# Whole 14 KB weight rows for the wide expert jobs of a one-core decoder trunk

## What is computed

```python
def swiglu(h, wg, wu, wd):
    return (jax.nn.silu(h @ wg) * (h @ wu)) @ wd

def moe_swiglu(h, router_w, wg, wu, wd):
    logits = (h @ router_w).astype(jnp.float32)
    top_val, top_idx = lax.top_k(logits, TOP_K)
    top_w = jax.nn.softmax(top_val, axis=-1)
    gates = jnp.sum(jax.nn.one_hot(top_idx, N_EXPERTS, dtype=jnp.float32) * top_w[..., None], axis=-2).astype(h.dtype)
    y = jnp.zeros_like(h)
    for e in range(N_EXPERTS):
        y = y + gates[..., e:e + 1] * swiglu(h, wg[e], wu[e], wd[e])
    return y
```

## Time and profile before

| | us |
|---|---|
| median of 3 runs | 1389.39 |
| lowest, highest | 1388.88, 1390.56 |
| the profiled execution, its own time | 1389.21 |
| its span, first to last instruction | 1387.4 |
| PE busy | 1370.8 (99%) |
| DVE busy | 806.9 (58%) |
| ACT busy | 663.1 (48%) |
| DMA read | 452.69 MB, 327 GB/s over the span |

### The profile page before, as it was taken

The page is one execution under the profiler, slowest core; times in us unless marked ns, Lnnn a source line. Parts: engine busy times, 40 slices in busy tenths (PEclk is TensorE's granted clock), DMA queues, the critical chain, the costliest instruction groups (busy, mean ns, idle before and its releaser), DMA issues.

```text
span 1387.4 us, 17886 instructions
## 1 busy us (share of the span) xinstructions
PE 1370.8 (99%) x6681; PEld 942.6 (68%) x6681; DVE 806.9 (58%) x1142; ACT 663.1 (48%) x886; POOL 10.3 (1%) x22
## 2 busy tenths in 40 slices
PE   9999999999999999999999999998999999999997
PEld 8887788888898877743435788434788535788432
DVE  5878666545458786631123999323899423999311
ACT  7657646444376485500012788212787212787210
POOL 2000000000000000000000000000000000000000
PEclk9999999999999999999999999999999999999999
DMA  9545446555544477899999999999999999999997
GB/s 352 194 173 183 154 144 220 182 187 194 176 156 160 159 273 284 310 404 426 406 429 420 422 422 426 430 431 420 421 422 429 430 430 420 421 423 428 430 429 296
DMA packets 105539, 454.91 MB, mean 328 GB/s; under 512 B 6440, under 2 KB 8752, under 8 KB 83696
## 3 DMA queue, kind: packets, MB, share of 16 engines
q1 hardware_dynamic: 104528, 452.47, 81.6%
q0 software_dynamic: 752, 1.23, 0.4%
q10 hardware_dynamic: 176, 0.07, 0.0%
HBM read 452.69 MB, written 1.06 MB: 327 GB/s over the span
## 4 chain that ended last, share of the span: by engine, by line
PE 87%; DMA 6%; DVE 3%; ACT 3%; issue 1%; DVEq 0%; ACTq 0%; SPq 0%
PE pA L841 39%; PE pB L841 19%; PE pB L1375 10%; PE pA L1375 8%; PE pA L1437 4%; DMA toep<-expert_w_gate_dram 4%; DMA late<-expert_w_down_dram 2%; PE pB L865 2%; PE pA L865 1%; DVE w_lo L1893 1%; ACT w_hi L1532 1%; PE pA L1294 0%; PE pB L1073 0%; ACT early_hi L1532 0%; PE pB L1254 0%
## 5 line engine op out<-in xcount | busy, mean ns | idle before, releaser
L1893 DVE TENSOR_TENSOR w_lo<-raw,w_hi 128x1024 fp32r<-128x1024 f32 x236 | 280.8, 1222 | 71.8 <-ACT w_hi L1532 68.9
L1532 ACT ACTIVATE w_hi<-raw 128x1024 fp32r<-128x1024 f32 x236 | 243.9, 1059 | 77.9 <-PE pB L841 38.5
L1893 DVE TENSOR_TENSOR w_lo<-late,w_hi 128x1024 fp32r<-128x1024 f32 x126 | 150.0, 1223 | 11.7 <-ACT w_hi L1532 6.0
L1532 ACT ACTIVATE w_hi<-late 128x1024 fp32r<-128x1024 f32 x126 | 132.4, 1061 | 33.0 <-PE pB L841 20.5
L1844 ACT ACTIVATE ex_act<-pA 64x512 f32<-64x512 f32 x15 | 8.9, 591 | 259.7 <-PE pA L1375 212.2
L1893 DVE TENSOR_TENSOR early_lo<-raw,early_hi 128x1024 fp32r<-128x1024 f32 x58 | 69.8, 1221 | 34.7 <-ACT early_hi L1532 34.6
L1375 PE MATMUL pB<-late,x_narrow 128*64 128x512 f32 x296 | 81.7, 592 | 0.0
L841 PE MATMUL pB<-w_hi,jT_hi 128*128 128x512 f32 x192 | 76.3, 397 | 2.5 <-DVE w_lo L1893 2.4
L2394 DVE TENSOR_TENSOR x<-pA,x 128x512 f32<-128x512 f32 x16 | 11.1, 692 | 116.2 <-PE pA L1295 116.2
L841 PE MATMUL pA<-w_hi,hT_hi 128*128 128x512 f32 x192 | 77.1, 402 | 0.0
L841 PE MATMUL pB<-w_hi,jT_lo 128*128 128x512 f32 x192 | 75.4, 393 | 0.0
(11 more groups left out here) (464 smaller groups left out, 2718.0 us busy)
## 6 DMA issues: line engine op xcount, KB each, us to landing
late<-expert_w_down_dram SPq DMA_DIRECT2D x46, 1024.0 KB, 19.8
raw<-w_in_dram SPq DMA_DIRECT2D x43, 1024.0 KB, 4.9
late<-expert_w_up_dram SPq DMA_DIRECT2D x29, 1024.0 KB, 18.4
first_run<-expert_w_gate_dram SPq DMA_DIRECT2D x16, 1792.0 KB, 16.0
first_run<-expert_w_up_dram SPq DMA_DIRECT2D x16, 1792.0 KB, 16.8
late<-expert_w_gate_dram SPq DMA_DIRECT2D x16, 1792.0 KB, 17.0
late<-expert_w_up_dram SPq DMA_DIRECT2D x16, 1792.0 KB, 17.7
raw<-expert_w_gate_dram SPq DMA_DIRECT2D x27, 1024.0 KB, 19.7
```

Of the source, the lines that this page charges most:

```text
L1532: f(halves_slot(m)[0], raw_slot(m), ACT.Copy).then_inc(s["w_hi_done"], 1)
L1893: tt(lo, raw_slot(m), hi.bitcast(F32), ALU.subtract).then_inc(s["w_lo_done"], 1)
```

## The change

Wide jobs take the same transfers as narrow ones, with all gate rows first, then all up rows, then the downs. The two lists come from one function, `job_items`. The piece order is written out by `wide_pieces`: for the gate matrix rows 0 to 3 in pairs (for each row the column pairs 0-1, 2-3, 4-5, then column chunk 6 of both rows as one piece of two runs of 512), then columns 0-1 of rows 4 to 7, then the rest of these rows in pairs; the same for up; then 28 down pieces. All seven gate sums stand in seven banks at once (B3, B1, B4, B5, B6, B7, B0), all seven Silu results in SBUF (six in the new `wide_acts` of 12 KB per partition, which lies over `low_slots` and `low_half`, used by job 0 alone, and the seventh in `ex_act`), and the up products take the same banks. Silus run at pieces 17, 19, 25, 25, 26, 27, 28, products at 45, 47, 53, 57, 59, 61, 63, transposes at 50, 57, 60, 64, 68, 72, 76. The scatter of the job before goes in four parts at pieces 8, 12, 16 and 20 through B2 alone, with the additions at 10, 14, 18 and 22. A ring place is free for the next load when the last piece of both rows of its pair is split. The cut diff:

```diff
+def job_items(narrow):
+
+    order = [("up" if r % 2 else "gate", r // 2) if narrow else ("up" if r // KT else "gate", r % KT) for r in range(ROWS)]
+    rows = [(unit, r // RUN_ROWS // 2, r // RUN_ROWS % 2, r % RUN_ROWS, r % RUN_ROWS * ROW, ROW)
+            for r, unit in enumerate(order)]
...
+def wide_pieces():
+
+    out = []
+    for kind in ("gate", "up"):
+        for k in range(0, RUN_ROWS, 2):
+            out += [(kind, k + r, c) for r in range(2) for c in (0, 2, 4)] + [(kind, k, SINGLE)]
+        out += [(kind, k, 0) for k in range(RUN_ROWS, KT)]
+        for k in range(RUN_ROWS, KT, 2):
+            out += [(kind, k + r, c) for r in range(2) for c in (2, 4)] + [(kind, k, SINGLE)]
+    return out + [("down", d // 4, d % 4) for d in range(4 * (FE // COLS))]
...
+        wide_acts = run_of.enter_context(nc.sbuf_tensor("wide_acts", [P, FE // COLS - 1, COLS], F32))
...
+        TURN_AT = [WIDE_ROWS - 6, WIDE_ROWS + 1, *(WIDE_ROWS + 4 * (c - 1) for c in range(2, SINGLE + 1))]
+        SILU_AT = [pieces.index(("gate", KT - 1, 0)) + n for n in (0, 2, 8, 8, 9, 10, 11)]
+        PRODUCT_AT = [pieces.index(("up", KT - 1, 0)) + n for n in (0, 2, 8, 12, 14, 16, 18)]
+
+        def w_bank(c):
+            return (B3, B1, B4, B5, B6, B7, B0)[c]
...
-                    sp.wait_ge(s["w_lo_done"], EX0 + FFE * wide_before(owner) + 2 * (RING * before + RUN * run + places[-1]) + 2)
+                    if before == 2:
+                        last = WIDE_ROWS + 2 * (RUN * run + places[-1]) + 1
+                    else:
+                        kind, k = items[False][RUN_ROWS * (2 * before + run) + (at + size - 1) // ROW][0]
+                        last = pieces.index((kind, k // 2 * 2, SINGLE))
+                    sp.wait_ge(s["w_lo_done"], EX0 + FFE * wide_before(owner) + last + 1)
...
-                if j and is_narrow(j):
-                    for (kind, c, *n), at_pass, run, slot, at, size in items:
+                if j:
+                    for (kind, c, *n), at_pass, run, slot, at, size in items[is_narrow(j)]:
...
             def job(j, w):
                 pe.wait_ge(s["n_x_ready"], w + 4)
                 pe.wait_ge(s["spread_ready"], j + 1)
...
+                for t, (kind, k, c) in enumerate(pieces):
+                    m = EX0 + t
                     if kind == "gate":
...
+                        pe.wait_ge(s["xg_lo_done"], 4 * w + k // 2 + 1)
+                    if kind == "up" and k < 2:
+                        pe.wait_ge(s["silu_done"], D0 + NCX * w + min(c + 2, NCX))
...
+                    elif c == SINGLE:
+                        chunk_piece(m, k // 2, COLS, [w_bank(c)], jT_hi, jT_lo, 1, j=w)
+                    else:
+                        row_piece(m, k, k == 0, [[w_bank(c), w_bank(c + 1)]], jT_hi, jT_lo, 1, w)
...
+                    if t in (8, 12, 16, 20):
+                        n = (8, 12, 16, 20).index(t)
+                        scatter_half(j - 1, n // 2, n % 2, False, 1)
```

More of the change, by code:

```diff
@@ L92, in ffn_order @@
     return order, at
[L95 to L107, removed]
 FOUR, TWO, SINGLE = (0, 1, 2, 3), (4, 5), 6
@@ L384, in program @@
         assert RING_SLOTS[PHASE] == ("toep", 0)
-        items = narrow_items()
-        item_at = {unit[:2]: place[:3] for unit, *place in items}
+        items = [job_items(narrow) for narrow in (False, True)]
+        item_at = [{unit[:2]: place[:3] for unit, *place in of_job} for of_job in items]
+        pieces = wide_pieces()
+        assert len(pieces) == FFE
         def ring_slot(kind, k):
@@ L407, in once_slot, with in_halves, unit_slot, unit_half @@
             return {"ex": once_ex, "ga": once_ga, "acts": once_acts}[name][:]
[L409 to L415, removed]
+        def in_halves(u):
+            return u in once and ONCE[once[u][0]][0] == "halves"
+        def unit_slot(u):
+            if u in once:
                 return once_slot(u)
-            return ring_slot(*RING_SLOTS[(ring_of_first[u] if first else PHASE + u) % RING])
-        def unit_half(u, h, first):
-            if in_halves(u, first):
+            return ring_slot(*RING_SLOTS[ring_of_first[u] % RING])
+        def unit_half(u, h):
+            if in_halves(u):
                 return (low_half, once_y)[h][:]
-            return unit_slot(u, first)[:, PIECE * h:PIECE * (h + 1)]
+            return unit_slot(u)[:, PIECE * h:PIECE * (h + 1)]
+        def wide_raw(t):
+            kind, k, c = pieces[t]
+            if kind == "down":
+                u = 2 * k + c // 2
+                return run_part(u // RUN, u % RUN * UNIT + PIECE * (c % 2), PIECE)
+            at_pass, run, slot = item_at[False][kind, k]
+            if c == SINGLE:
+                both = run_part(run, slot * ROW, 2 * ROW).rearrange("p (r n) -> p r n", r=2)
+                return both[:, :, COLS * SINGLE:]
+            return run_part(run, slot * ROW + COLS * c, PIECE)
+        def like_raw(m, part):
+            if m >= EX0 and pieces[m - EX0][2] == SINGLE and pieces[m - EX0][0] != "down":
+                return part.rearrange("p (r n) -> p r n", r=2)
+            return part
         def raw_slot(m):
@@ L476, in program @@
         assert n == FFD
[L477 to L478 removed]
+        assert len(EXPERT_W) == SINGLE + 1
         def ends(order):
@@ L491, in turns, with wide_act @@
             return at
[L493 to L519, removed]
+        TURN_AT = [WIDE_ROWS - 6, WIDE_ROWS + 1, *(WIDE_ROWS + 4 * (c - 1) for c in range(2, SINGLE + 1))]
[3 more added lines that the diff above has]
+            return (B3, B1, B4, B5, B6, B7, B0)[c]
+        def wide_act(c):
+            return ex_act[:, 0] if c == SINGLE else wide_acts[:, c]
         def turn_bank(c):
-            return (B6, B7)[c % 2] if c else B4
+            return (B1, B4)[c % 2]
         def load_pair_count(eng):
```

162 lines of the change are left out of this document (60 added, 102 removed).

## The result

The changed kernel takes **1405.08 us** (median of four runs, 1403.87 to 1416.04) against 1389.48 (1388.88 to 1390.56) before: a ratio of 1.0129, with a 95% interval of 1.0078 to 1.0180. It is 15.6 us slower where 2.5 us less was predicted. The run of 1416.04 had a mean granted clock of 0.944, the other three 0.995 to 0.996. The profiled execution took 1405.76 us, with a span of 1404.0.

A forecast was written before the change was run, and what follows sets the result against it. DMA (208.0 us a pair of jobs) was taken to bound, PE almost level (204.94). Start +1.7 less 1.3 of waits gives +0.4; less 2.9, -2.5 on 1389.21, plus 0.18 to the median: 1386.9 us, range 1383.3 to 1390.5.

The forecast's parts named there:

- The start of a wide job: First wide job waits for whole rows 0 and 1: +1.13, +0.2 and +0.4, together +1.7 us, paid once.
- PE in a wide job: Matmul and transpose counts in wide jobs unchanged, so 0 us, bounds -0.5 to +0.5.
- Covered: Scatters at pieces 8 to 20 share one bank; 1.36 x 2 us are left for an addition's 1.06 + 0.69.
- The loads: Wide jobs' weights come in 103.0 us instead of 105.0, 2.0 us a job; last weights land 6.0 us earlier.
- Removable waits: PE's waits for down weights, 1.3 us in the first narrow job and 2.9 in the last: 4.2 us.
- The loop's gap stays: The 2.42 us gap ahead of the second wide job belongs to PE's loop branch, not weights, and remains.
- The low clock stays: Granted clock of 0.60 for 4 us behind the loop's gap remains; that wide job is 1.56 us longer.
- Rivals 1 and 2: Loop gap ahead of second wide job: 1 shrinks with slow clock, 1383.5 us, 11%; 2 grows by 1.7, 1388.6 us, 15%.
- ACT and DVE: In wide jobs the same operations at moved places: 0 us, bounds -0.2 to +2 us a job.
- rival 3: ACT becomes the bound at pieces 25 to 33 and 57 to 63: +5.7 us, 1392.6 us, chance 11%.
- Release by pairs: A slot's next load waits for both rows of a pair; queue stays filled, cost 0, bounds 0 to 2 us.
- Rival 4: Larger rows bring nothing: wide jobs' loads stay at 105.0 us, total 1389.5 us, chance 8%.

The follow-up runs named there:

- e1_order: Changed kernel with rows 4 and 5 of gate and up taken as a pair, columns 0-1 ahead only for rows 6 and 7; 1388.79 us.
- e2_scatter_late: Changed kernel with its own piece order, scatters moved to pieces 29, 33, 37, 41 and additions to 31, 35, 39, 43; 1407.27 us.
- e3_short_rows: Changed kernel loading only the first quarter of the columns of gate rows 4 to 7 in each wide job; 1388.69 us.
- e7_paired_scatter: Changed kernel in e1_order's piece order, both scatter halves side by side in two banks after pieces 23 and 25; 1385.38 us.
- e4_quarter_runs: e1_order with each wide gate and up row loaded as four transfers of 3.5 KB runs; 1390.20 us.
- e6_before_light: Kernel before, with half of each wide down weight not loaded; 1382.69 us.
- e5_all_pairs: Changed kernel with all eight rows in pairs, no columns ahead, Silus and products moved to suit; 1403.04 us (two runs).
- e8_three_ahead: e7_paired_scatter with three pieces, not four, split ahead of the copy of the narrow job's output; 1385.04 us.

## Why the prediction was wrong, step by step

- **The start of a wide job (+1.7): near at its place, and stopped too early.** Worked out were +1.13 for PE's first matmul, +0.2 and +0.4; measured are +1.73 for the first matmul (760.69 where 760.09 was worked out) and 0.4 at piece 3, 2.1 in all. The kernels with the new loads start between 759.92 and 760.72, so part of the difference is spread. But the step followed the landing of rows 0 and 1 only. Its own numbers were enough to see the stall. With row 0 at 757.71 and 4.27 us a row, row 6 lands at 783.3 and is ready 2.38 later, at 785.7; row 7 at 787.6 and 790.0. PE, started at 760.09, is through sixteen pieces of 1.36 at 781.9, or 783.6 with two scatter halves of 0.89 (measured), and wants row 6 there, 2.1 us too early; it wants row 7 one piece and one half on, at 785.9, 4.1 us too early. The trace has PE at row 6's piece at 786.38 and at row 7's at 793.20. Of the 7.3 us lost in this job these numbers give 4.1 and the low clock 1.5; the rest I don't divide further (ACT's copy of row 7 begins at 789.14 where 787.6 was worked out, and DVE's addition goes ahead of the scatter). **This is the step that failed**: it took the wait for rows 4 to 7 at nothing, and 17.3 us hang on it, more than the 16.6 of the whole (after against e1_order, 7.3 + 2.1 + 7.9; e2_scatter_late and e3_short_rows bear out the cause).
- **PE in a wide job (0, bounds -0.5 to +0.5): wrong, +1.75 us a job, 5.2 in the sum.** "No term changes" counted scatter matmuls, eight before and after, not the places where they interrupt the pieces: two before, four after, at 0.76 + 0.13 us each. e7_paired_scatter takes 1.7 us back in each of the first two jobs. The prediction's "Covered" for the scatters at 8 to 20 holds for the waits where rows are on time (e1_order has none there), but not for the scatters themselves; and in the change the addition that piece 16's scatter needs stood behind a subtraction for row 7, which the 1.06 + 0.69 us of that sum left out.
- **The loads (2.0 us a job): right.** Wide loads run at 430 GB/s once PE keeps up (e1_order, 752.5 to 857.5 us), at 416 to 420 with 3.5 KB runs (e4_quarter_runs). Within the change they only reached 408 from 765 to 855 us, for want of free places. (The slices at 9 tenths begin at 590 us, 17 of 34.7, and not at 622 as the prediction has it; nothing hangs on it.)
- **Removable waits (4.2 us): mis-sized.** 6.0 us in e6_before_light's span. After also got all of it: narrow jobs and the end gave back 6.5 us. Six waits of the brackets hid 1.9 us more, 0.3 each.
- **The loop's gap stays: right. The low clock stays: wrong in this profile,** which gives 1.6 us back. The branch takes 5925 ns in after and 5825 to 6301 in the experiments, the gap 1.9 to 2.4 us. Rivals 1 and 2 both fall as they were put: of rival 1 only the low clock's part came, and the gap is 2.02 where it was 2.42.
- **ACT and DVE (0), and rival 3: right that it costs nothing.** PE has no wait at pieces 25 to 33 or 57 to 67 in any kernel but e5_all_pairs, whose order delays the products. The slower side came by another way than the one rival named for it.
- **Release by pairs (0 us, and the queue stays filled): the cost is right, the reason is not.** The prediction named a DMA share under 1.0 about 1090 us as a sign that the queue runs dry. It came, in after (0.95 from 1096 to 1112 us) and in e1_order, where there is no stall:

```profile
1084.00:1100.00 16.00, 16.00 (x74) 8.66 (x75) 5.42 (x6) 3.59 (x5) 0.00 (x0) 1.00 0.94 378
```

  The kernel before has 430 GB/s in the same 16 us, and its shortest time from issue to landing there is 11.9 us, e1_order's 8.2. So the queue did run low behind the second wide job, and that narrow stage came at 419 GB/s in place of 428 (1065.5 to 1168.5 us). It cost PE nothing: no matmul waits in it. e7_paired_scatter, with the same release, has 407 GB/s there, and e6_before_light, with the old one and fewer bytes to load, 391, so the release by pairs isn't shown to be the cause; no run separates it. In the first wide stage e1_order stands at 1.01, so after's 0.98 there was of the stall.
- **Rival 4 (rows bring nothing): falls**, by e4_quarter_runs.

The sum with measured terms: start +1.7 and +0.4 at piece 3, order +17.3, halves +5.2, low clock -1.6, narrow jobs and end -6.5. Together +16.5, against +16.6 measured. The range failed because every part of it was a bound on a term that I had listed. A stall by order was none of them. That the loads came out as predicted helped nothing: the forecast of a gain rested on wide jobs of unchanged length.

## What to carry to other kernels

When the order of loads or of their use changes, write both down side by side for the whole job: the time at which each unit is ready, and that at which the engine reaches it. The average rate says nothing on a stretch that takes one piece from each of four units in a row. A larger unit needs a consumer that spends at least the unit's load time on it: here three and a half pieces of 1.36 us for a row of 4.27 us did, and one piece didn't. Small operations that break a stream of matmuls are to be counted by their interruptions, not by their matmuls.

## What the runs showed of the hardware that I had not expected

**Two halves cost as much as one.** PE's rows of the kernel before at a scatter of both halves (four matmuls of 64 rows, in the two halves of the array and in two banks), and then those of the kernel after at one half (two matmuls):

```profile
779.76 0.39 PE L841 MATMUL pA<-w_hi,jT_lo 128*128 128x512 f32 x1
780.08 0.50 PE L1306 MATMUL pB<-y_hi,spread 64*128 64x512 f32 x2
780.42 0.40 PE L1306 MATMUL pB<-y_lo,spread 64*128 64x512 f32 x2
780.75 0.50 PE L841 MATMUL pA<-w_hi,jT_hi 128*128 128x512 f32 x1
```

```profile
773.47 0.39 PE L837 MATMUL pB<-w_hi,jT_lo 128*128 128x512 f32 x1
773.79 0.50 PE L1289 MATMUL pA<-y_hi,spread 64*128 64x512 f32 x1
774.13 0.40 PE L1290 MATMUL pA<-y_lo,spread 64*128 64x512 f32 x1
774.45 0.50 PE L837 MATMUL pB<-w_hi,jT_hi 128*128 128x512 f32 x1
```

From the last matmul ahead to the first behind it is 0.99 us with four and 0.98 with two. With the piece behind, a scatter adds 0.89 us (2.12 + 1.49 less two pieces of 1.36), whether of one half or of both. The Trainium skill (TensorEngine Tiling (Array Packing), "Theoretical Speedup") gives up to twice the speed with two tiles where a small dimension is 64 or less; by these rows the trace agrees, with the full factor.

**A stall is paid twice, at times.** 4 us without a matmul were followed by a granted clock of 0.57 in the next 4 us, and a piece of 2.60 in place of 1.49 us. Behind the loop's gap of some 2 us it goes either way: 0.60 before (gap 2.42), 0.59 in e8_three_ahead and low as well in four more experiments, 1.00 after (2.02), in e1_order (2.40), e7_paired_scatter (2.21) and two more. The gap's length alone doesn't decide it, and what does stays open. It is worth 1.5 us of one profile, as much as several of the edits here.

**Brackets undercount PE's waits.** Six waits of 4.2 us by the rows gave 6.1 us when they were removed. In the narrow jobs four matmuls take 1.08 us and eight 1.89, so a pair side by side takes 0.41, while one alone is listed with 0.59: the listed end lies 0.18 us behind the time at which the next could start, and idle time counts only from there. The other 0.1 us of each wait stays open. The Trainium skill (Perfetto Trace Analysis, "Summary: the profiler window per engine type") says that the end of a TensorE instruction is estimated; the trace agrees.

**A releaser in a bracket may itself have been waiting.** [4.08 <-DVE x] was a row of weights that hadn't landed, two engines up; e2_scatter_late, without any scatter there, lost as much.
